# Router products on the residual, selection inside the modulation loop, and the last modulation units moved into attention

## The reference, cut to what matters

```
mod = silu(c) @ w_mod[l] + b_mod[l]            # six vectors: shift1, scale1, gate1, shift2, scale2, gate2
y  = attention of two kinds (8 heads with a local bias from na_rpb, 4 heads without) @ od_w_out
x  = x + gate1 * rmsnorm(y, g[l,1])
h  = rmsnorm(x, g[l,2]) * (1 + scale2) + shift2
logits = h @ router_w                          # 8 experts
gates = softmax of the two largest logits
x  = x + gate2 * rmsnorm(sum over experts of gate_e * (silu(h @ w1_e) * (h @ w3_e)) @ w2_e, g[l,3])
```

## Time and profile before

| what | value |
| --- | --- |
| median of 3 runs (lowest to highest) | 1917.74 us (1915.91 to 1919.04) |
| the profiled execution: its own time, its span | 1918.83 us, 1916.9 us |
| busy share of the span: PE, DVE, ACT, POOL | 96%, 66%, 56%, 1% |
| mean granted clock of PE | 0.978 of full |
| attention of layer 1 (first scores to first odo product) | 811.4 to 874.6 us of the span |
| odo products | 874.6 to 899.4 us |
| from there to the first product of expert unit 0, and of unit 2 | 935.8 us, 943.6 us |
| experts, to the last store | to 1916.9 us |

### The profile page before, as it was taken

The page is one execution under the profiler, slowest core; times in us unless marked ns, Lnnn a source line. Parts: engine busy times, 40 slices in busy tenths (PEclk is TensorE's granted clock), DMA queues, the critical chain, the costliest instruction groups (busy, mean ns, idle before and its releaser), DMA issues.

```text
span 1916.9 us, 23184 instructions
## 1 busy us (share of the span) xinstructions
PE 1834.1 (96%) x9604; PEld 1488.2 (78%) x9604; DVE 1267.6 (66%) x1185; ACT 1076.1 (56%) x1099; POOL 25.8 (1%) x27
## 2 busy tenths in 40 slices
PE   6998798999999989989999999999999999999998
PEld 4876476888888868747788888888888888888886
DVE  4334724323333364174788989889898898988987
ACT  5322535322232244364777777777777777777775
POOL 0000000000000001030000000000000000000000
PEclk9998899999999999999799999999999999999999
DMA  9654063623232354242799999999989999999994
GB/s 315 201 160 130 19 223 111 197 90 109 88 102 96 94 184 125 88 121 72 258 375 371 362 373 332 372 371 360 387 326 379 372 363 378 337 363 373 359 371 180
DMA packets 263216, 473.89 MB, mean 247 GB/s; under 512 B 16120, under 2 KB 115376, under 8 KB 263104
## 3 DMA queue, kind: packets, MB, share of 16 engines
q1 hardware_dynamic: 262720, 471.38, 69.4%
q0 software_dynamic: 384, 0.95, 0.3%
HBM read 471.25 MB, written 1.05 MB: 246 GB/s over the span
## 4 chain that ended last, share of the span: by engine, by line
PE 90%; DVE 5%; ACT 2%; DMA 1%; issue 1%; SPq 1%; POOL 0%; DVEq 0%; ACTq 0%
PE bank L535 27%; PE bank L537 26%; PE bank L536 26%; PE bank L602 1%; PE bank L2142 1%; PE bank L2105 1%; DMA raw_weights<-in_ev_w_in 1%; PE bank L405 1%; PE bank L392 1%; PE bank L803 1%; DVE overlay L476 1%; PE bank L885 1%; DVE residual L488 1%; PE bank L911 1%; ACT split_high L514 1%
## 5 line engine op out<-in xcount | busy, mean ns | idle before, releaser
L1652 DVE TENSOR_TENSOR split_low<-raw_weights,split_high 128x2048 fp32r<-128x2048 f32 x224 | 513.0, 2290 | 43.1 <-ACT split_high L1406 42.0
L1406 ACT ACTIVATE split_high<-raw_weights 128x2048 fp32r<-128x2048 f32 x222 | 426.2, 1920 | 139.9 <-PE bank L537 139.9
L519 DVE TENSOR_TENSOR split_low<-raw_weights,split_high 128x1024 fp32r<-128x1024 f32 x118 | 144.8, 1233 | 290.4 <-ACT split_high L514 290.2
L535 PE MATMUL bank<-h_high,split_high 128*128 128x512 f32 (+1 forms) x832 | 316.9, 381 | 8.6 <-DVE h_low L449 5.2
L536 PE MATMUL bank<-h_low,split_high 128*128 128x512 f32 (+1 forms) x832 | 314.5, 378 | 0.0
L537 PE MATMUL bank<-h_high,split_low 128*128 128x512 f32 (+1 forms) x832 | 314.4, 378 | 0.0
L1652 DVE TENSOR_TENSOR h_low<-raw_weights,h_high 128x2048 fp32r<-128x2048 f32 x112 | 256.8, 2292 | 53.8 <-ACT h_high L1406 52.5
L535 PE MATMUL bank<-split_high,xe_high 128*128 128x512 f32 x672 | 266.3, 396 | 0.0
L537 PE MATMUL bank<-split_high,xe_low 128*128 128x512 f32 x672 | 262.2, 390 | 0.0
L536 PE MATMUL bank<-split_low,xe_high 128*128 128x512 f32 x672 | 261.9, 390 | 0.0
L1406 ACT ACTIVATE h_high<-raw_weights 128x2048 fp32r<-128x2048 f32 x112 | 214.9, 1918 | 49.9 <-PE bank L537 49.9
(11 more groups left out here) (279 smaller groups left out, 2458.2 us busy)
## 6 DMA issues: line engine op xcount, KB each, us to landing
raw_weights<-in_moe_w SPq DMA_DIRECT2D x336, 1024.0 KB, 6.7
raw_weights<-in_w_mod SPq DMA_DIRECT2D x48, 1024.0 KB, 7.1
raw_weights<-in_ffn_w SPq DMA_DIRECT2D x33, 1024.0 KB, 5.3
raw_weights<-in_ev_w_in SPq DMA_DIRECT2D x10, 1024.0 KB, 9.5
raw_weights<-in_od_w_in SPq DMA_DIRECT2D x8, 1024.0 KB, 7.0
raw_weights<-in_ev_w_out SPq DMA_DIRECT2D x4, 1024.0 KB, 9.0
raw_weights<-in_od_w_out SPq DMA_DIRECT2D x4, 1024.0 KB, 9.2
overlay<-in_rpb SPq DMA_DIRECT2D x32, 64.0 KB, 2.4
```

What stands on the lines that cost most here:

```text
L519: dve.tensor_tensor(half_of(s, j, SPL[:, s % NSPLIT, :]), half_of(s, j, raw_of(split_at[s])), half_of(s, j, SPH[:, s % NSPLIT, :]).bitcast ...
L535: pe.matmul(ps, wh, xh, start=first, stop=False)
L1406: act.activation(esplit(u)[0], RAW[:, u % NRAW, :], ACT.Copy).then_inc(S("e_high"), 1)
L1652: dve.tensor_tensor(lo, RAW[:, u % NRAW, :], hi.bitcast(F32), ALU.subtract).then_inc(S("e_low"), 1)
```

## The change

Four edits go together.

1. In the list of units, mod units 44 to 47 stand before the four odo units and not behind them. The two places of `load_bias` are bound to the same named units as before (mod unit 42, third odo unit).
2. The hooks of attention take all four pairs: PE rows at i = 0 to 3, turns at 1 to 4; ACT copies at i = 1 to 4; at i = 3 PE waits for ACT's copy of pair 23; DVE's additions, both scale vectors and a new tensor `router_gained` (router weights times the norm's scale) stand at i = 5. The rows and turns behind odo go.
3. The router's products are made from the residual and `router_gained` while the residual is updated. What the shift vector adds is a product of its own (8 matmuls of 8 columns before n5's spread), and the root of each token comes by two products of one column. DVE combines them in `selection(0)`. The selection's three steps stand inside `dve_modulate`, after tiles 0, 1 and 2. DVE's diagonals of gate2 (L1646) stand ahead of n6's reciprocal.
4. ACT makes the high parts of the tokens before those of expert units 0 and 1; the gate's exponential with its two table loads stands in the experts' loop, behind the high parts of units 2 and 3. DVE makes the low part of expert unit 0 after the first one-hots, that of unit 1 between the low parts of the gathered tokens. PE makes both `gain_rows` after the dispatch of the first two experts.

```diff
-    units += mods(40, 44)
+    units += mods(40, 48)
     units += [("split", "odo", cols(w["od_w_out"][0], 256 * s)) for s in range(4)]
-    units += mods(44, 48)
...
@@ dve_modulate
-        def dve_modulate(dve, n, c0, full=False, first=None):
+        def dve_modulate(dve, n, c0, full=False, first=None, between=lambda t: None):
...
                 if t + 2 < nt:
                     tmp(t + 2)
+                between(t)
...
@@ ACT
-                if i in (1, 2):
+                if i in (1, 2, 3, 4):
                     act_mods(act, 19 + i, 20 + i, 5)
...
             act_root(act, N["n5"])
-            act_mods(act, 22, 24, 5)
...
             for f in range(2):
-                act.wait_ge(S(f"eraw{f}"), 16)
-                act.activation(esplit(f)[0], RAW[:, f, :], ACT.Copy).then_inc(S("e_high"), 1)
                 act.wait_ge(S("htok_full"), f + 1)
                 for t in range(2):
                     act.activation(HTH[:, t, 512 * f:512 * f + 512], PS[2 * t + f][:, :], ACT.Copy)\
                        .then_inc(S("htok_high"), 1)
+            for f in range(2):
+                act.wait_ge(S(f"eraw{f}"), 16)
+                act.activation(esplit(f)[0], RAW[:, f, :], ACT.Copy).then_inc(S("e_high"), 1)
...
                         if i == 1 and e == 0:
+                            if b == 0:
+                                gate_exponential()
                             onehot_turned()
...
@@ DVE
-                if i == 3:
-                    dve_mods(dve, 10, 11, 6)
-                    dve_affine(dve, 1, 2, 1.0, 32)
+                if i == 5:
+                    dve_mods(dve, 10, 12, 6)
+                    link(dve, dve_affine(dve, 1, 2, 1.0, 32))
+                    dve_affine(dve, 1, 3, 0.0, 40).then_inc(S("affine"), 1)
+                    dve.wait_ge(S("router_in"), 16)
+                    dve.tensor_tensor(RWA[:, :, :], RW[:, :, :], VEC[:, 1, 2, :, 1:2].to_broadcast([P, KT, NE]),
+                                      ALU.mult).then_inc(S("router_gain"), 1)
...
+                if step == 0:
+                    dve.wait_ge(S("logits"), 1)
+                    dve.wait_ge(S("token_rs"), 1)
+                    link(dve, dve.tensor_copy(RT[:, 160:170], PS[7][:, 0:10]))
+                    for t in range(2):
+                        last = dve.scalar_tensor_tensor(LG[:, t, :], PS[4 + t][:, 0:8], RTOK[:, t:t + 1], SHR,
+                                                        ALU.mult, ALU.add)
+                    link(dve, last)
...
+            dve_modulate(dve, N["n6"], 256, True, None, selection)
...
-                if b == 0:
-                    dve.wait_ge(S("e_high"), 2)
-                    low_of(1)
-                for r in range(4):
-                    xe_low(0, r)
+                for f in range(2):
+                    if b == 0:
+                        dve.wait_ge(S("e_high"), f + 1)
+                        low_of(f)
+                    xe_low(0, 2 * f)
+                    xe_low(0, 2 * f + 1)
...
@@ PE
-                if i < 2:
-                    if i == 1:
-                        pe_mod_turn(pe, 20, 6)
+                if 1 <= i <= 4:
+                    pe_mod_turn(pe, 19 + i, 6)
+                if i < 4:
                     pe_mod_rows(pe, 40 + 2 * i, 5)
                     pe_mod_rows(pe, 41 + 2 * i, 5)
-                if i == 2:
-                    pe_mod_turn(pe, 21, 6)
+                if i == 3:
+                    pe.wait_ge(S("mod_rows"), 24)
                 if i == 5:
-                    pe.wait_ge(S("mod_evac"), 11)
+                    pe.wait_ge(S("mod_evac"), 12)
...
-            pe_mod_rows(pe, 44, 5)
-            pe_mod_rows(pe, 45, 5)
+            pe.wait_ge(S("router_gain"), 1)
+            for k in range(KT):
+                pe.matmul(PS[7][:, 0:8], MOD[:, 1, 24 + k, 1:2].to_broadcast([P, P]), RW[:, k, :],
+                          start=(k == 0), stop=(k == KT - 1))
             pe_spread(pe, N["n5"])
-            pe_mods(pe, 46, 48, 5, 7, turned=22)
-            pe_sums(pe, N["n6"])
+
+            def logits(k):
+
+                pe.wait_ge(*nsem("n5", "res", k + 1))
+                for t in range(2):
+                    last = pe.matmul(PS[4 + t][:, 0:8], X[:, k, CTX + P * t:CTX + P * t + P], RWA[:, k, :],
+                                     start=(k == 0), stop=(k == KT - 1))
...
+            logits(0)
+            for k in range(KT):
+                if k + 1 < KT:
+                    logits(k + 1)
+                pe_sum(pe, N["n6"], k)
             pe_spread(pe, N["n6"])
...
                 for r in range(4):
                     dispatch(0, r)
+                if b == 0:
+                    pe.wait_ge(S("grow_diag"), 1)
+                    gain_rows(0)
+                    gain_rows(1)
```

More of the change, by code:

```diff
@@ L1354, in _, with gate_exponential @@
                        .then_inc(S("htok_high"), 1)
[L1356 to L1359, removed]
+            for f in range(2):
+                act.wait_ge(S(f"eraw{f}"), 16)
+                act.activation(esplit(f)[0], RAW[:, f, :], ACT.Copy).then_inc(S("e_high"), 1)
+            def gate_exponential():
+                act_table(act, ACT.Exp, 51)
+                act.wait_ge(S("top_diff"), 1)
+                act.activation(RT[:, 64:66], RT[:, 66:68], ACT.Exp).then_inc(S("top_exp"), 1)
+                act_table(act, ACT.Silu, 52)
             def experts(b):
@@ L1647, in _ @@
             last.then_inc(S("grow_diag"), 1)
[L1649 to L1655, removed]
+            dve.wait_ge(*nsem("n5", "res", KT))
+            dve_rstd(dve, N["n6"])
             LG, MX = RT[:, 0:16].rearrange("p (t e) -> p t e", t=2), RT[:, 16:32].rearrange("p (t e) -> p t e", t=2)
@@ L1665, in _ @@
             POS = RT[:, 144:160].rearrange("p (t e) -> p t e", t=2)
[L1666 to L1675, removed]
@@ L1676, in _ @@
-            dve.tensor_tensor(DIF, MX[:, :, 1], MX[:, :, 0], ALU.subtract).then_inc(S("top_diff"), 1)
-            link(dve, dve.tensor_copy(IF, IX))
-            iota8 = CON[:, C_IOTA:C_IOTA + NE]
[L1679 to L1683, removed]
+            SHR, RTOK = RT[:, 160:168], RT[:, 168:170]
@@ new lines, in _, with selection @@
+            iota8 = CON[:, C_IOTA:C_IOTA + NE]
+            def selection(step):
+                if step == 0:
[6 more added lines that the diff above has]
+                    link(dve, last)
+                if step == 1:
+                    for t in range(2):
+                        last = dve.max(MX[:, t, :], LG[:, t, :])
+                    link(dve, last)
+                    for t in range(2):
+                        last = dve.max_index(IX[:, t, :], MX[:, t, :], LG[:, t, :])
+                    link(dve, last)
+                if step == 2:
+                    dve.tensor_tensor(DIF, MX[:, :, 1], MX[:, :, 0], ALU.subtract).then_inc(S("top_diff"), 1)
+                    link(dve, dve.tensor_copy(IF, IX))
+                    for t in range(2):
+                        dve.tensor_scalar(T1[:, t, :], iota8, IF[:, t, 0:1], None, ALU.is_equal)
+                        last = dve.tensor_scalar(T2[:, t, :], iota8, IF[:, t, 1:2], None, ALU.is_equal)
+                    link(dve, last)
+                    dve.tensor_tensor(SEL, T1, T2, ALU.add).then_inc(S("selected"), 1)
@@ L1685, in _, with low_of @@
+            dve_modulate(dve, N["n6"], 256, True, None, selection)
+            def low_of(u):
+                hi, lo = esplit(u)
+                dve.tensor_tensor(lo, RAW[:, u % NRAW, :], hi.bitcast(F32), ALU.subtract).then_inc(S("e_low"), 1)
             for i in range(4):
@@ L2055, in _ @@
                 pe.wait_ge(*nsem("n6", "h", k + 1))
-                for t in range(2):
-                    last = pe.matmul(PS[4 + t][:, 0:8], HFULL[:, k, P * t:P * t + P], RW[:, k, :],
-                                     start=(k == 0), stop=(k == KT - 1))
-                if k == KT - 1:
-                    last.then_inc(S("logits"), 1)
                 for t in range(2):
@@ L2071, in gain_rows @@
                   .then_inc(S("grow_full"), 1)
-            pe.wait_ge(S("grow_diag"), 1)
-            gain_rows(0)
             pe.wait_ge(S("selected"), 1)
@@ L2081, in _ @@
             pe.matmul(PS[5][:, 16:24], ones, SEL[:, 1, :], start=False, stop=True).then_inc(S("positions"), 1)
-            gain_rows(1)
             pe.wait_ge(S("htok_low"), 4)
```

15 lines of the change are left out of this document (8 added, 7 removed).

## The result

| | median (range, runs) | ratio to before |
| --- | --- | --- |
| before | 1918.32 us (1915.91 to 1919.15, 5) | |
| changed | 1944.88 us (1940.3 to 1947.7, 5) | 1.0135 [1.0124, 1.0147] |

The profiled execution of the changed kernel took 1946.43 us, with a span of 1944.6 and a mean granted clock of 0.970 (before: 1918.83, 1916.9, 0.978). It is slower, as forecast, but by 26.6 us and not by 18.4, and the median lies just above the range. (The 1917.74 that the forecast started from is the median of the first three of these five runs.) PE holds 90% of the chain as in the earlier trace rows.

A forecast was written before the change was run, and what follows sets the result against it. PE was taken to bound 90% of the chain. SP's order 11.9, four pairs in attention 6.2 and everything behind odo 0.3 made 18.4 us on the median 1917.74: 1936.1 us forecast, range 1926 to 1943.

The forecast's parts named there:

- Where the path goes: Attention: the chain runs through late bias 2, PE at half clock, the new hooks, and unit 5's adds waiting for turn 23.
- The order of SP's stream: Attention: bias 2 waits for mod 42 and 43's buffers and stands behind two 1 MB odo loads, delaying unit 2's adds 11.9 us.
- the walk: The prediction's step-by-step timing of attention: 8.3 us for buffer waits alone, bias 2's last issue at 823.7, landing by 829.7.
- the upper bound: Attention: SP's issues stall behind the loads for 2 us and the clock returns some 3 us later, making attention 23 us longer.
- Four pairs: Attention's hooks: the moved mod pairs' rows and turns, partly at half clock, add another 6.2 us.
- Behind odo, +0.3 to T: From the last odo evacuation to T, n6's first scaled tile: the last product pair and two sums cost 0.3 us.
- The product pairs per tile fit in the 0.85 of a tile: Residual loop: PE's new router products for each tile fit within DVE's 0.85 us a tile.
- T to dispatch 11.5, to unit 2 29.4: From n6's first scaled tile: dispatch after 11.5 us (today 16.8), unit 2's low part after 29.4 (today 30.0); gain shrinks to 0.6.
- The clock once more before unit 2, 0 to 1.7: Before expert unit 2: PE idles some 3 us, which may drop its clock again and cost 0 to 1.7 us.
- Sum: Whole kernel: 11.9 + 6.2 + 0.3 = 18.4 us slower, 1936.1 us on the median.
- A deeper loss: Rival: issues stall and the clock comes back late, in attention and before expert unit 2: 23 + 3 us, 1944, chance 0.13.
- small DMAs pass the loads: Rival, attention: bias 2 isn't held behind odo's loads, SP's order costs 8.3 us, PE keeps its clock: 1929, chance 0.22.

The follow-up runs named there:

- e5: The changed kernel with biases 2 and 3 loaded ahead of mod unit 46 and all later biases ahead of odo's loads: 1929.6 us, ratio 1.0061.
- e1: The changed kernel with bias 2's four copies ahead of the first two odo loads, still behind the buffer waits: 1942.1 us, ratio 1.0138.
- e6: The kernel before with only the new mod pairs moved into attention, router and gates as before: 1935.6 us, ratio 1.0094.
- e8: The changed kernel with the shift's products behind n6's spread, 16 unused products in their place and 16 behind n5's spread: 1944.9 us, ratio 1.0142.
- e7: The kernel before with the router's part alone, gates' exponential early, shift's products behind n6's spread, gate2's diagonals behind the first one-hots: 1923.7 us, ratio 1.0035.
- e4: The changed kernel with the gates' exponential and its table switches back at their old, earlier place on ACT: 1940.6 us, ratio 1.0126.
- e2: The changed kernel with bias 2's copies ahead of mod unit 46, later biases still ahead of the third odo load: 1937.1 us, ratio 1.0110.
- e3: The changed kernel with 64 unused products added, 32 ahead of the shift's products and 32 behind n5's spread: 1947.6 us, ratio 1.0165.
- e10: The changed kernel with biases in the old order, gates' exponential early, and unused products in PE's waits from the first logits to the dispatch: 1928.2 us, ratio 1.0063.
- e12: The kernel before with unused products: 2 behind each n6 sum, 8 behind the last, fewer than e9 behind the spread and in tiles: 1916.6 us, ratio 0.9995.
- e9: The kernel before with unused products: 4 behind each n6 sum, 16 behind the last, others behind spread, transposes and gain rows: 1914.9 us, ratio 0.9995.

## Why the prediction was right in direction and short in size

- **Where the path goes.** Right: bias 2, the half clock behind it, the order of the hooks and the wait for turn 23 are in the chain as walked.
- **The order of SP's stream, 11.9.** 13.9 by e5, 14.0 at the adds. The wait for buffers was right (8.4 by e1, 8.3 in the walk). The other share was 5.6 and not 3.6. The landing came as forecast (5.87; 823.7 to 829.7 in the walk), but the first issue took 2.58 instead of 0.61, which I had kept for the upper bound only. The Trainium skill's rule on ring order ("DMA: Bandwidth & Descriptors", Queues, rings and completion order) agrees, and e1's landing of 2.30 shows the other side of it.
- **Four pairs, 6.2.** In the changed kernel the adds of unit 5 come 19.5 later and those of unit 2 14.0, which leaves 5.5. e5 measures 5.8 with the bias on time. How much of either is half clock was not measured. That the rest of attention goes on as before holds within 0.3.
- **Behind odo, +0.3 to T.** This is the step that failed. "The product pairs per tile fit in the 0.85 of a tile" holds, nearly, at full clock only (0.88 measured). I had moved four units of rows and two turns away and kept in the clock's bill only the places where PE already idled. With that work in place the clock stayed up through the residual loop; with that work alone moved away (e6) it fell in the loop. In the changed kernel it fell at 925 and the loop became PE's, 1.52 a tile: 5.98 in place of 0.3. e8 shows 4.0 of it to be the clock's, and in e6, at half clock but without the logits, the stretch is only 0.2 longer; the rest is not split. Nor would the old place of the pairs have saved the loop: e7 has them there and loses the same, by logits that start 2.6 later and a clock that falls at the fourth sum.
- **T to dispatch 11.5, to unit 2 29.4.** 11.0 and 29.0. The shape (gain shrinks to 0.6 because the exponential is late) was right, 0.9 measured. The next activation followed the table load's 1.28 at once again (964.14, 965.43), so that the 2.66 of the Trainium skill ("ScalarE: Activation LUTs", What ACT_TABLE_LOAD costs) is not seen here either.
- **The clock once more before unit 2, 0 to 1.7.** It did fall: 1.5. The sum left 0.6 for it; e4 shows that it is the late gate's.
- **Sum.** 18.4 forecast; 19.75 + 5.98 - 0.94 + 1.49 = 26.3. Of the gap of 7.9, the residual loop is 5.7 and attention 1.65.
- **The rivals.** "A deeper loss" (1944) has the right number and two of its parts (issues that stall, clock before unit 2), but it does not have the residual loop, which is the largest part of the gap. So the number is luck. That small DMAs pass the loads is refuted by e1 and e2.

## What to carry to other kernels

When dense products are moved out of a stretch, recompute what stays there at half clock, above all loops that run close to another engine's pace: 0.88 beside 0.85 looks free and becomes 1.52. A small transfer belongs ahead of the large loads in its queue; when one is rescued, look at the next small one at once (e2). And split a change in halves early: here each half was slower by itself (e6, and e7 with its differences).

## What the runs showed that I had not expected

- A DMA issue was not a fixed cost: behind two 1 MB issues SP's 64 KB issue took 2.58 and 3.01 us instead of 0.61, and in e2 the second of two 1 MB issues took 4.18.
- In the changed kernel the clock fell right behind the shift's products, though they had kept PE busy for 1.88 us. In e8, with 32 dense products around the same wait and no products of the shift there, it stayed at 1.00. In e3 dense products stood on both sides of the shift's and it fell all the same. But in e10, with the shift's products in place and 16 dense ones behind them, it stayed at 1.00 until the fourth sum. So they don't bring it down every time, and what decides where it falls stays open.
- In e7 the clock fell 5 us behind the last of the pairs' rows although PE had no gap: it made turns, logits and sums.
- Fillers between the sums were not free although DVE sets the pace of the loop: T came 1.3 later with two behind each sum (e12) as with four (e9), since PE had been catching up there.
